# The opening of a two-layer diffusion trunk on one core: the first pair of projection tiles moved ahead of the second block's modulation sums, the third tile computed beside them

## The chip, the core and the metric

The kernel runs on one core of one Trainium2 chip. The metric is device time in microseconds (us) for one execution of the whole program; the time before is the median of three runs. Five engines each work through an instruction queue of their own and wait for one another by semaphores: TensorE (PE, matmuls; PEld is its weight load), VectorE (DVE), ScalarE (ACT), GpSimd (POOL) and SyncE (SP, which issues most of the DMAs).

## What is computed

One inference step of a trunk of two layers (`DEPTH` 2) over 128 context tokens and 512 latent tokens, with 1024 features, in float32. The part that matters here is the start of the first layer:

```python
def trunk_layer(x, cond, ctx_k, ctx_v, p):
    sh1, sc1, gt1, sh2, sc2, gt2 = modulation(cond, p['w_mod'], p['b_mod'])
    h = rms_norm(x, p['norm1_g']) * (1.0 + sc1) + sh1
    q, k, v, u = mixer_projections(h, p['w_in'], p['q_norm_g'], p['k_norm_g'])
...
def modulation(cond, w_mod, b_mod):
    m = jax.nn.silu(cond) @ w_mod + b_mod
    return jnp.split(m[:, None, :], N_MOD, axis=-1)
...
def mixer_projections(h, w_in, q_norm_g, k_norm_g):
    proj = h @ w_in
...
```

After it come attention, a pooling mixer, an output projection and a gated MLP; then the second layer, and a final norm.

## The kernel before

Features lie on the partitions: `x` is 8 blocks k of 128 features by 640 tokens. A projection is made in tiles of 128 output features. The input projection of a layer has 10 tiles: four of u (tiles 0 to 3), then k, v and four of q. Each float32 operand is split into a high and a low part, and a product is made of three: high by high, low weights by high input, high weights by low input. For one block k and one tile each of them is two matmuls, of 384 and 256 tokens ("a product" below is such a pair of matmuls).

ACT makes the high part of the weights (`w_hi`, by `hi`, L658) and DVE the low part (`w_lo`, by `lo`, L1027), from the raw weights (`w_raw`, two slots, filled by SP). `w_hi` and `w_lo` have two slots as well: the parts of tile n+2 replace those of tile n, so `hi` of tile n+2 waits until tile n is finished. Tile 2 has a place of its own in memory that the attention uses later (`k_hi`, `k_lo`).

The opening of layer 0 works like this.

- PE transposes the tokens of `x` (L1742) into two PSUM places, DVE and ACT copy the results out. ACT sums squares, and PE spreads the reciprocal root mean square of each token over the partitions (L1629). DVE multiplies `x` by it, block by block (`scaled_x`, L1200).
- The shift and the scale of the norm come from 8 MB of weights, in 4 blocks f of 256 features of each. For a block PE makes the sums in two halves (`first_sums(f, h)`, L1703, a block's half needs 1 MB of weights, `w_first`, loaded in two DMAs), ACT copies the row (L784), PE turns it into columns (`first_columns(f)`, L1714), and DVE adds these up to the shift and gain of features 2f and 2f+1 (`first_mod(f)`, L1206 to L1212). Only then can ACT make the normed input of these two blocks k (L797, "sq", then its high part `in_hi`, L801) and DVE the low part (`in_lo`, L1232).
- PE then makes tiles 0 and 1 together (`linear_pair`): for each k the high products, then the low ones, with the sums of later blocks in between and `first_columns(k//2+1)` in the middle of k = 0, 2 and 4. Tile 2 follows alone (`linear_third`), then the first of eight small steps for other modulations (`mod_second(0)`, L1720), then tile 3 (`linear`, L1468) and on.

SP issues the loads in the order of the program: tokens, block 0 of `w_first`, tiles 0 and 1, blocks 1 to 3, tiles 2 and 3, constants.

Of the kernel before, what the change touches and what calls it, by code (L numbers as in the profile page):

```python
# [21 lines left out]
P = 128  # L22
# [39 lines left out]
def build(nc, x_prompt, x_sample, cache_k, cache_v, c, c_ctx, w_mod, b_mod, norm1_g, w_in,  # L62
# [72 lines left out]
    with ExitStack() as ctx:  # L135
# [15 lines left out]
        cst = sb("cst", [P, n_const])  # L151
        ident, head_ones, ones = (cst[:, i * P:(i + 1) * P] for i in range(3))
        cos, sin = (cst[:, 3 * P + i * TS:3 * P + (i + 1) * TS] for i in range(2))
        fold = cst[:, n_const - P:n_const]
        edge = cst[:, 3 * P + 2 * TS:n_const - P].rearrange("p (g s e c) -> p g s e c", g=NPOOL, s=2, e=2)
# [4 lines left out]
        eps = sb("eps", [P, 2])  # L160
        wp = sb("wp", [P, NPOOL, P])
# [25 lines left out]
        XE_SCALAR, XE_VECTOR = [4, 6], [0, 1, 2, 3, 5, 7]  # L187
# [77 lines left out]
        s_xhat = sem("x_scaled")  # L265
# [104 lines left out]
        def own_place(n):  # L370

            t = n % PER_LAYER
            if t == 2:
                return w_third_in
            return w_own_up[2 * (t - N_IN - N_OUT):2 * (t - N_IN - N_OUT) + 2]

# [14 lines left out]
        def _(sp):  # L391
# [25 lines left out]
            def load_second(k):  # L417
                if k == 0:
                    sp.wait_ge(s_xsq, NT)
                elif k == 1:  # L420
                    sp.wait_ge(s_fcol, NK // 2)
                else:
                    sp.wait_ge(s_second, k - 1)
# [22 lines left out]
            sp.dma_start(cst[:, P:n_const - P], consts[:, P:n_const - P]).then_inc(s_const, 16)  # L446
            load_second(0)
            load_second(1)
            for L in range(DEPTH):
# [79 lines left out]
        def _(pool):  # L529
# [32 lines left out]
            pool.memset(cond_cols, 0.0).then_inc(s_c32z, 1)  # L562
            for L in range(DEPTH):
# [14 lines left out]
                if L == 0:  # L578
                    pool.wait_ge(s_const, 16)
# [22 lines left out]
                for e in range(NE):  # L602
                    E = L * NE + e
                    tgt = keys[:, TP + PAST:TP + PAST + TS] if e == 0 else qk[:, e % 3, TP:T]
                    if E > 0:
                        pool.wait_ge(s_qk, E)
                    pool.wait_ge(s_shuf, E + 1)
# [44 lines left out]
        def _(act_e):  # L652
# [7 lines left out]
            def slot_loads(n, s):  # L660
                return n // 2 + 1 if isinstance(n, int) else (n - s) // 2 + 1

            def hi_own(n):

                s = n % 2
                act_e.wait_ge(s_raw[s], 16 * slot_loads(n, s))
                act_e.activation(own_place(n)[0], w_raw[:, s, 0:NK, :], ACT.Copy).then_inc(s_whi, 1)

            def hi_at(base, i, s, nk):

                act_e.wait_ge(s_raw[s], 16 * (i + (base // 2 + 1)))
# [99 lines left out]
            act_e.activation(rtok[:, :], rtok[:, :], ACT.Sqrt, bias=eps[:, 0:1], scale=1.0 / D).then_inc(s_sd, 1)  # L771
            for k in XE_SCALAR:
                act_e.wait_ge(s_xt, k + 1)
                act_e.activation(x[:, k, :], pair[k % 2][:, 0:T], ACT.Copy).then_inc(s_xe, 1)
            hi(0, 0, NK)


            for k in range(NK):
                if k == 0 or k % 2 == 1 and k + 1 < NK:
                    f = (k + 1) // 2  # L780
                    act_e.wait_ge(s_mfirst, f + 1)
                    if f >= 2:
                        act_e.wait_ge(s_fcol, f - 1)
                    act_e.activation(first_rows[:, f % 2, :], pair[2][:, f % 2 * 512:(f % 2 + 1) * 512], ACT.Copy).then_inc(s_frow, 1)  # L784
                if k == 0:
                    for L in range(DEPTH):
                        act_e.wait_ge(s_vec_t, L + 2)
                        for t in range(3):
                            ins = act_e.activation(vec[:, L, t, 0:N_ROWS[t]], pair[L][:, t * P:t * P + N_ROWS[t]], ACT.Copy)
                        ins.then_inc(s_vec, 1)  # L790
                    hi(1, 1, NK)
# [1245 lines left out]
```

## Time and profile before

| | us |
|---|---|
| median of 3 runs | 1442.25 (1441.65 to 1442.99) |
| span of the profiled execution, first to last instruction | 1439.4 |
| start of the first product of the projection | 29.87 |
| start of tile 3 | 59.86 |

The profile shows one execution. Its own time is known as the span; the 2.85 us by which the median exceeds it lie around the first and last instruction. Times in the trace count from the first instruction. A busy PE there is not PE at its peak, since matmuls overlap.

### The profile page before, as it was taken

The numbers are of one execution on the slowest core, as the hardware profiler recorded it, in microseconds if no ns is written. First come the engines' busy times: TensorE is split into PE (matmuls) and PEld (weight loads), VectorE is DVE, ScalarE is ACT, GpSimd is POOL, SyncE is SP. The second block draws the span as 40 slices with busy tenths as digits, with TensorE's granted clock in tenths as the row PEclk, the third lists the DMA queues.
The fourth block names the chain that finished last, engine by engine and source line by source line (L and its number), as shares of the span: only waits on it lengthen the run. The fifth ranks groups of instructions, "written<-read, shape, count | busy, mean of one in ns | idle before, by whom it ended". The sixth has DMA issues, their size and how long they took to land.

```text
span 1439.4 us, 25053 instructions
## 1 busy us (share of the span) xinstructions
PE 1407.3 (98%) x9905; PEld 1353.2 (94%) x9905; DVE 903.1 (63%) x1429; ACT 534.1 (37%) x798; POOL 400.5 (28%) x273
## 2 busy tenths in 40 slices
PE   6999999999999999999999999999999999999997
PEld 4888889999999999999999977999999999999997
DVE  4448869897966478785775787369744323444333
ACT  5436862533231123232242587344233112232322
POOL 0264002153440033433205800214433101323321
PEclk9999999999999999999999999999999999999999
DMA  9752005253535334335423200224323312222321
GB/s 315 248 178 80 1 2 161 81 166 106 164 121 162 94 117 145 120 120 153 120 58 86 63 1 2 59 89 132 104 79 90 87 57 67 73 73 73 101 61 74
DMA packets 198158, 147.05 MB, mean 102 GB/s; under 512 B 4400, under 2 KB 187448, under 8 KB 197048
## 3 DMA queue, kind: packets, MB, share of 16 engines
q1 hardware_dynamic: 196592, 144.27, 32.8%
q10 hardware_dynamic: 1480, 1.57, 0.3%
q8 instruction: 61, 1.00, 0.3%
q14 instruction: 25, 0.20, 0.0%
HBM read 142.94 MB, written 2.88 MB: 101 GB/s over the span
## 4 chain that ended last, share of the span: by engine, by line
PE 87%; DVE 7%; ACT 2%; issue 2%; SPq 1%; DMA 1%; DVEq 0%; ACTq 0%
PE pair L1468 68%; PE pair L1484 7%; PE pair L1865 3%; PE pair L1910 3%; PE pair L1879 2%; DVE mod_acc L1050 1%; DVE in_lo L1116 1%; DVE norm_t L1106 1%; SPq L414 1%; DVE conv L1390 1%; DMA w_first<-in_w_mod_dram 1%; DVE w_lo L1027 1%; DVE small L1328 1%; PE pair L1768 1%; PE pair L1720 1%
## 5 line engine op out<-in xcount | busy, mean ns | idle before, releaser
L1468 PE MATMUL pair<-in_hi,w_hi 128*128 128x384 f32 x1728 | 396.1, 310 | 0.2
L1468 PE MATMUL pair<-in_lo,w_hi 128*128 128x384 f32 x1728 | 394.7, 309 | 0.0
L1468 PE MATMUL pair<-in_hi,w_lo 128*128 128x384 f32 x1728 | 392.7, 308 | 0.0
L1390 DVE SCALAR_TENSOR_TENSOR conv<-pair,vec,conv 128x127 f32<-128x127 f32 x352 | 168.7, 541 | 193.4 <-ACT conv L935 192.9
L1468 PEld LDWEIGHTS pair<-in_hi,w_hi 128*128 128x128 f32 x1728 | 265.4, 189 | 5.6 <-issue 2.2
L1468 PEld LDWEIGHTS pair<-in_lo,w_hi 128*128 128x128 f32 x1728 | 265.6, 189 | 0.0
L1468 PEld LDWEIGHTS pair<-in_hi,w_lo 128*128 128x128 f32 x1728 | 263.6, 188 | 0.0
L636 POOL TENSOR_TENSOR silu_a<-silu_a,conv 128x640 f32<-128x640 f32 x44 | 113.0, 2567 | 534.2 <-DVE conv L1390 534.2
L935 ACT ACTIVATE conv<-pair,vec 128x640 f32<-128x640 f32 x88 | 77.8, 886 | 407.5 <-PE pair L1468 405.3
L1027 DVE TENSOR_TENSOR w_lo<-w_raw,w_hi 128x1024 fp32r<-128x1024 f32 (+1 forms) x148 | 195.7, 1322 | 38.4 <-ACT w_hi L658 37.9
L658 ACT ACTIVATE w_hi<-w_raw 128x1024 fp32r<-128x1024 f32 (+1 forms) x82 | 96.9, 1182 | 287.1 <-PE pair L1468 270.5
L1050 DVE SCALAR_TENSOR_TENSOR mod_acc<-mod_raw,cond,mod_acc 128x1024 f32<-128x1024 f32 x112 | 181.5, 1666 | 0.0
L1183 DVE SCALAR_TENSOR_TENSOR x<-pair,mod,x 128x128 f32<-128x128 f32 x80 | 40.3, 545 | 165.4 <-PE pair L1468 165.4
L1468 PE MATMUL pair<-act_lo,w_hi 128*128 128x384 f32 x616 | 140.7, 309 | 0.0
L1468 PE MATMUL pair<-act_hi,w_hi 128*128 128x384 f32 x616 | 140.3, 309 | 0.0
L1468 PE MATMUL pair<-act_hi,w_lo 128*128 128x384 f32 x616 | 140.1, 308 | 0.0
L547 POOL TENSOR_TENSOR ssum<-ssum,sq 128x640 f32<-128x640 f32 x24 | 48.6, 2025 | 300.7 <-ACT sq L682 300.7
L1468 PEld LDWEIGHTS pair<-act_lo,w_hi 128*128 128x128 f32 x616 | 94.8, 189 | 0.0
L1468 PEld LDWEIGHTS pair<-act_hi,w_hi 128*128 128x128 f32 x616 | 94.5, 188 | 0.0
L1468 PEld LDWEIGHTS pair<-act_hi,w_lo 128*128 128x128 f32 x616 | 94.1, 188 | 0.0
L640 POOL TENSOR_TENSOR act_lo<-silu_a,act_hi 128x640 f32 x44 | 84.4, 1918 | 7.5 <-POOL act_hi L638 7.5
L673 ACT ACTIVATE w_hi<-w_raw 128x1024 fp32r<-128x1024 f32 x64 | 67.2, 1050 | 0.0
(205 smaller groups left out, 1775.5 us busy)
## 6 DMA issues: line engine op xcount, KB each, us to landing
w_raw<-in_w_up_dram SPq DMA_DIRECT2D x88, 512.0 KB, 3.8
mod_raw<-in_w_mod_dram SPq DMA_DIRECT2D x64, 512.0 KB, 4.4
w_raw<-in_w_down_dram SPq DMA_DIRECT2D x32, 704.0 KB, 4.6
w_raw<-in_w_in_dram SPq DMA_DIRECT2D x20, 512.0 KB, 4.2
w_first<-in_w_mod_dram SPq DMA_DIRECT2D x16, 512.0 KB, 8.8
w_raw<-in_w_out_dram SPq DMA_DIRECT2D x16, 512.0 KB, 4.1
mod_raw<-in_w_mod_dram SPq DMA_DIRECT2D x4, 1024.0 KB, 5.1
mod_acc<-in_w_mod_dram SPq DMA_DIRECT2D x4, 1024.0 KB, 5.0
```

Source lines behind the costliest of these rows:

```text
L547: pool.tensor_tensor(ssum[:, :], ssum[:, :], sq_slot(m), ALU.add).then_inc(s_ss, 1)
L636: pool.tensor_tensor(silu_a[:, :], silu_a[:, :], conv[:, 1, :], ALU.mult).then_inc(s_act, 1)
L640: pool.tensor_tensor(act_lo[:, j, :], silu_a[:, :], act_hi[:, j, :].bitcast(F32), ALU.subtract).then_inc(s_alo, 1)
L658: act_e.activation(w_hi[:, s, 0:nk, :], w_raw[:, s, 0:nk, :], ACT.Copy).then_inc(s_whi, 1)
L673: act_e.activation(w_hi[:, s, 0:nk, :], w_raw[:, s, 0:nk, :], ACT.Copy).then_inc(s_whi, 1)
L935: act_e.activation(conv[:, s, :], up_result(g, j, s), ACT.Identity, bias=v(L, V_CONVB, s * NF + g * FG + j), scale=v(L, V_TAP[1], s * NF + ...
L1027: dve.tensor_tensor(w_lo[:, s, 0:nk, :], w_raw[:, s, 0:nk, :], w_hi[:, s, 0:nk, :].bitcast(F32), ALU.subtract).then_inc(s_wlo, 1)
L1050: dve.scalar_tensor_tensor(out=mod_acc[:, ci, :], in0=mod_raw[:, s, :], scalar=cond[:, ci, ds(k, 1)], in1=mod_acc[:, ci, :], op0=ALU.mult, ...
L1390: ins = dve.scalar_tensor_tensor(out=conv[:, s, d0:d1], in0=up_result(g, j, s)[:, d0 + sh:d1 + sh], scalar=v(L, V_TAP[t], s * NF + g * FG ...
L1468: ins = pe.matmul(dst[:, a:e], w[:, s, k, :], rhs[:, kk, a:e], start=first and r == 0, stop=last and r == 2)
L1484: ins = pe.matmul(dst[:, a:e], w, rhs[:, a:e], start=start, stop=stop)
L1865: ins = pe.matmul(lin[i % 2][:, oc:oc + n], q_st[:, h, b * P:(b + 1) * P], kk[:, h // GRP, kc:kc + n], start=r == 0, stop=r == 1)
```

## The change

The work of the first 60 us is put in another order, and some of it into other places. No arithmetic is removed but for the filler matmuls, which become 12 instead of 6.

- **Loads.** Tile 2's raw weights go to a place of their own (half of `mod_raw`) and are issued behind block 1 of `w_first`, ahead of blocks 2 and 3. Its two parts (`third_hi`, `third_lo`) lie where the rotation tables (`turn`) and the past keys and pool weights lie later, so these loads wait for the end of tile 2.
- **Transposes.** Three PSUM places instead of two; the sums of block 0 and the first half of the vectors stand between and behind the last transposes, ahead of the spreading of the norm. ACT copies the spread norm to `spread_x`, and `scaled_x` reads it there.
- **Weights.** GpSimd makes the high part of tile 1. On DVE the low part of tile 0 comes behind `first_mod(0)`, that of tile 1 behind the first `in_lo`, that of tile 2 behind `first_mod(1)`.
- **PE.** k = 0 of tiles 0 and 1 comes ahead of both halves of block 1's sums; then k = 1 with `first_columns(1)` in its middle; then k = 0 and 1 of tile 2; from k = 2 on the three tiles go together, with `first_columns(2)` and `first_columns(3)` in the middle of k = 3 and k = 5. Behind k = 7 come at once `mod_second(0)` and tile 3.
- **PSUM.** Sums of blocks 1 to 3 lie in `pair[3]` instead of `pair[2]`, which tile 2 now needs.

```diff
@@ SP
-            for f in range(1, NK // 2):
+            sp.wait_ge(s_xsq, 4)
+            load_first(1)
+            sp.dma_start(third_raw, w_in_v[0][:, :, IN_COLUMN[2]:IN_COLUMN[2] + P]).then_inc(s_third, 16)
+            for f in range(2, NK // 2):
                 load_first(f)
-            for n in range(2, 4):
-                load_in(0, n)
...
+            load_in(0, 3)
...
+            sp.wait_ge(s_lin, 3)
+            sp.dma_start(turn[:, :], consts[:, 3 * P:3 * P + 2 * TS]).then_inc(s_turn, 16)
@@ GpSimd
+            pool.wait_ge(s_raw[1], 16)
+            pool.wait_ge(s_whi, 1)
+            pool.tensor_copy(w_hi[:, 1, 0:NK, :], w_raw[:, 1, 0:NK, :]).then_inc(s_whi, 1)
@@ ScalarE
+            first_copied(0)
+            act_e.wait_ge(s_bc, 1)
+            act_e.activation(spread_x, lin[3], ACT.Copy).then_inc(s_spread, 1)
             hi(0, 0, NK)
+            vec_copied(1)
...
+                if k % 2 == 1 and k + 1 < NK:
+                    first_copied((k + 1) // 2)
+                if k == 1:
+                    hi_own(2)
@@ VectorE
-            dve.wait_ge(s_bc, 1)
-            for k in range(2):
-                scaled_x(k)
-            lo(0, 0, NK)
+            dve.wait_ge(s_spread, 1)
+            scaled_x(0)
...
             first_mod(0)
-            lo(1, 1, NK)
+            lo(0, 0, NK)
+            scaled_x(1)
             for k in range(NK):
+                dve.wait_ge(s_hhi, 2 * (k + 1))
+                dve.tensor_tensor(in_lo[:, k, :], sq[:, k % 2, :], in_hi[:, k, :].bitcast(F32), ALU.subtract).then_inc(s_h, 2)
+                if k == 0:
+                    lo(1, 1, NK)
                 if k + 2 < NK:
                     scaled_x(k + 2)
                 if k % 2 == 1 and k + 1 < NK:
                     first_mod((k + 1) // 2)
...
+                if k == 1:
+                    lo(2, 0, NK)
...
-                    if L == 0 or n > 0:
+                    if n > 0:
                         lo(N + 2, n % 2, NK)
@@ TensorE
+            first_sums(0, 1)
             pe.wait_ge(s_rstd, 1)
+            x_emptied(5)
             spread_tiles(range(NT)).then_inc(s_bc, 1)
...
             first_columns(0)
+            vec_turned(1)
...
+            keep_busy(12, pair[0][:, 0:P])
...
-                    linear_pair(tile_in(L), NK, in_hi, in_lo, *h_wait(2 * L), first_ahead, first_between)
-                    linear_third(tile_in(L) + 2, NK, in_hi, in_lo, lin[2])
+                    opened_hi(0, (0, 1))
+                    opened_lo(0, (0, 1))
+                    first_sums(1, 0)
+                    first_sums(1, 1)
+                    opened_hi(1, (0, 1))
+                    first_columns(1)
+                    opened_lo(1, (0, 1))
...
+                    for k in range(2):
+                        opened_hi(k, (2,))
+                        opened_lo(k, (2,))
+                    first_sums(2, 0)
+                    opened_hi(2, (0, 1, 2))
+                    opened_lo(2, (0, 1, 2))
+                    first_sums(2, 1)
+                    opened_hi(3, (0, 1, 2))
+                    first_columns(2)
+                    opened_lo(3, (0, 1, 2))
+                    first_sums(3, 0)
+                    opened_hi(4, (0, 1, 2))
+                    opened_lo(4, (0, 1, 2))
+                    first_sums(3, 1)
+                    opened_hi(5, (0, 1, 2))
+                    first_columns(3)
+                    opened_lo(5, (0, 1, 2))
+                    for k in range(6, NK):
+                        opened_hi(k, (0, 1, 2))
+                        opened_lo(k, (0, 1, 2))
+                    pe.wait_ge(s_fsum, NK // 2)
                     mod_second(0)
```

`opened_hi(k, tiles)` makes the two products with the high input of each tile, and waits at k = 0 for the low part of that tile's weights; `opened_lo` makes the one with the low input, and at k = 7 tells that the tile is finished.

**Where the order moves.** First, PE's queue at the last columns (block 3; the names are PSUM place, then input and weights, then the shape; in brackets the semaphores waited for). Before, in the middle of k = 4:

```order
L1714 MATMUL pair2<-cst,mod_acc 128x128 [waits first_rows_copied]
L1714 MATMUL pair2<-cst,mod_acc 128x128 x3
L1484 MATMUL pair0<-in_lo,w_hi 128x384 [waits h_ready]
L1484 MATMUL pair0<-in_lo,w_hi 128x256
L1484 MATMUL pair1<-in_lo,w_hi 128x384
L1484 MATMUL pair1<-in_lo,w_hi 128x256
L1484 MATMUL pair0<-in_hi,w_hi 128x384 [waits h_hi_ready]
```

Now, in the middle of k = 5:

```order
L1741 MATMUL pair3<-cst,mod_acc 128x128 [waits first_rows_copied]
L1741 MATMUL pair3<-cst,mod_acc 128x128 x3
L1541 MATMUL pair0<-in_lo,w_hi 128x384 [waits h_ready]
L1541 MATMUL pair0<-in_lo,w_hi 128x256
L1541 MATMUL pair1<-in_lo,w_hi 128x384
L1541 MATMUL pair1<-in_lo,w_hi 128x256
L1541 MATMUL pair2<-in_lo,third_hi 128x384
L1541 MATMUL pair2<-in_lo,third_hi 128x256
L1541 MATMUL pair0<-in_hi,w_hi 128x384 [waits h_hi_ready]
```

The last row of the first piece is k = 5, whose features come from block 2; that of the second is k = 6, whose features come from these very columns.

Second, DVE's queue from the spreading of the norm to the low part of tile 1 (`xin` is the scaled `x`; L1200 is now L1254, L1027 is L1081, L1232 is L1281). Before:

```order
L1200 TENSOR_TENSOR xin<-x,pair3 128x640 [waits x_evacuated_by_vector,rstd_spread]
L1200 TENSOR_TENSOR xin<-x,pair3 128x640 [waits x_evacuated_by_vector]
L1027 TENSOR_TENSOR w_lo<-w_raw,w_hi 128x1024 [waits w_hi_ready]
L1221 SCALAR_TENSOR_TENSOR first_gain<-vec 128x8 [waits vec_ready]
L1206 TENSOR_REDUCE first_sum<-pair2 128x8 [waits first_columns_done,first_gain_ready]
```

Now:

```order
L1254 TENSOR_TENSOR xin<-x,v_feat 128x640 [waits x_evacuated_by_vector,rstd_copied]
L1273 SCALAR_TENSOR_TENSOR first_gain<-vec 128x8 [waits vec_ready]
L1260 TENSOR_REDUCE first_sum<-pair2 128x8 [waits first_columns_done,first_gain_ready]
...
L1081 TENSOR_TENSOR w_lo<-w_raw,w_hi 128x1024 [waits w_hi_ready]
L1254 TENSOR_TENSOR xin<-x,v_feat 128x640 [waits x_evacuated_by_vector]
L1281 TENSOR_TENSOR in_lo<-sq,in_hi 128x640 [waits h_hi_ready]
L1081 TENSOR_TENSOR w_lo<-w_raw,w_hi 128x1024 [waits w_hi_ready]
```

The second row of L1081 is the low part of tile 1; it now has one scaling, `first_mod(0)`, the low part of tile 0, a second scaling and the first low input ahead of it.

Third, DVE's queue behind the last low input, where the tiles of u are copied out of PSUM (L1294 and L1295, now L1351 and L1352) and the low part of tile 3 is made. Before:

```order
L1294 COPY u<-pair0 128x128 [waits pads_cleared,lin_done]
L1295 COPY u<-pair0 128x512
L1025 TENSOR_TENSOR k_lo<-w_raw,k_hi 128x1024 [waits w_hi_ready]
L1294 COPY u<-pair1 128x128 [waits lin_done]
L1295 COPY u<-pair1 128x512
L1027 TENSOR_TENSOR w_lo<-w_raw,w_hi 128x1024 [waits w_hi_ready]
```

Now:

```order
L1351 COPY u<-pair0 128x128 [waits pads_cleared,lin_done]
L1352 COPY u<-pair0 128x512
L1351 COPY u<-pair1 128x128 [waits lin_done]
L1352 COPY u<-pair1 128x512
L1081 TENSOR_TENSOR w_lo<-w_raw,w_hi 128x1024 [waits w_hi_ready]
```

L1025, tile 2's low part, has left this place; the last row, tile 3's low part, still follows the copies of tiles 0 and 1. Before, PE had all of tile 2 to do after those two tiles were finished; now the three are finished together.

## Rows read from the trace of the kernel before

**Rows 1.** The page: the chain that ended last, its shares by engine.

```profile
PE 87%; DVE 7%; ACT 2%; issue 2%; SPq 1%; DMA 1%; DVEq 0%; ACTq 0%
```

**Rows 2.** Chain in order of time, opening: start us, us, what.

```profile
22.87 10.00 DMA w_first<-in_w_mod_dram
...
43.89 1.20 ACT sq L797 x2
...
45.17 0.75 ACT in_hi L801
...
45.96 12.98 PE pair L1484 x84
```

**Rows 3.** Timeline, PE: start us, us, operation; in brackets idle before, releaser.

```profile
24.18 1.60 PE L1654 MATMUL pair<-cst 128*128 128x128 f32 x12
...
28.87 1.06 PE L1703 MATMUL pair<-w_first,ssum 128*32 128x512 f32 x8 [1.94 <-DMA w_first<-in_w_mod_dram]
29.87 0.56 PE L1484 MATMUL pair<-in_hi,w_hi 128*128 128x384 f32 x2
...
32.91 1.07 PE L1703 MATMUL pair<-w_first,ssum 128*32 128x512 f32 x8 [0.55 <-DMA w_first<-in_w_mod_dram]
...
39.30 1.06 PE L1703 MATMUL pair<-w_first,ssum 128*32 128x512 f32 x8
...
42.26 1.07 PE L1703 MATMUL pair<-w_first,ssum 128*32 128x512 f32 x8
...
44.54 0.60 PE L1714 MATMUL pair<-cst,mod_acc 128*128 128x128 f32 x4
...
45.96 0.56 PE L1484 MATMUL pair<-in_hi,w_hi 128*128 128x384 f32 x2 [0.23 <-ACT in_hi L801]
...
51.73 0.46 PE L1484 MATMUL pair<-in_hi,k_hi 128*128 128x384 f32 x2
...
58.87 1.06 PE L1720 MATMUL pair<-mod_raw,ssum 128*32 128x512 f32 x8
59.86 0.56 PE L1468 MATMUL pair<-in_hi,w_hi 128*128 128x384 f32 x2
```

**Rows 4.** Timeline, DVE, columns as in rows 3.

```profile
20.73 1.55 DVE L1200 TENSOR_TENSOR xin<-x,pair 128x640 f32<-128x640 f32 x2 [0.29 <-PE pair L1629]
...
24.28 0.19 DVE L1206 TENSOR_REDUCE first_sum<-pair 128x8 f32<-128x32 f32 x1 [0.47 <-PE pair L1714]
...
25.15 1.22 DVE L1027 TENSOR_TENSOR w_lo<-w_raw,w_hi 128x1024 fp32r<-128x1024 f32 x1
...
45.17 0.19 DVE L1206 TENSOR_REDUCE first_sum<-pair 128x8 f32<-128x32 f32 x1 [1.97 <-PE pair L1714]
...
45.54 0.28 DVE L1212 TENSOR_SCALAR gain<-first_sum,vec,first_gain 128x2 f32<-128x2 f32 x1
...
51.63 0.29 DVE L1294 COPY u<-pair 128x128 f32<-128x128 f32 x1 [0.90 <-PE pair L1484]
...
52.44 1.22 DVE L1025 TENSOR_TENSOR k_lo<-w_raw,k_hi 128x1024 fp32r<-128x1024 f32 x1
...
54.37 1.52 DVE L1027 TENSOR_TENSOR w_lo<-w_raw,w_hi 128x1024 fp32r<-128x1024 f32 x1
```

**Rows 5.** Timeline, ACT: a copy of 640 tokens from PSUM.

```profile
18.59 0.70 ACT L774 ACTIVATE x<-pair 128x640 f32<-128x640 f32 x1 [0.85 <-PE pair L1742]
```

**Rows 6.** Groups by form, POOL: the nearest copies; xcount | busy us, mean ns | idle before.

```profile
L638 POOL CAST act_hi<-silu_a 128x640 f32 x44 | 45.6, 1036 | 7.3 <-POOL silu_a L636 7.3
```

**Rows 7.** Timeline, POOL: the first window sum.

```profile
52.70 2.11 POOL L591 TENSOR_TENSOR tree<-u 128x663 f32<-128x663 f32 x1 [9.04 <-DVE u L1295]
```

**Rows 8.** Stretch 25 to 30 us: PE, PEld, DVE, ACT, POOL busy, clock, DMA share, GB/s.

```profile
25.00:30.00 5.00, 2.98 (x25) 1.04 (x24) 3.65 (x6) 1.90 (x4) 0.00 (x0) 1.00 1.09 348
```

**Rows 9.** The page: DMA issues, KB each, us to landing.

```profile
w_raw<-in_w_in_dram SPq DMA_DIRECT2D x20, 512.0 KB, 4.2
```

More of the change, by code:

```diff
@@ L160, in build @@
         eps = sb("eps", [P, 2])
+        with ExitStack() as own:
+            third_lo = sb("third_lo", [P, NK, P], F32R, at=own)
         wp = sb("wp", [P, NPOOL, P])
@@ L606, in _ @@
                         pool.wait_ge(s_qk, E)
+                    else:
+                        pool.wait_ge(s_turn, 16)
                     pool.wait_ge(s_shuf, E + 1)
@@ L1734, in x_emptied, with vec_turned @@
                     pe.wait_ge(s_xe_dve, XE_VECTOR.index(k) + 1)
+            def vec_turned(L):
+                if L > 0:
+                    pe.wait_ge(s_vec, L)
+                for t in range(3):
+                    ins = pe.transpose(vec_place(t), rows[0:N_ROWS[t], L, t, :], ident[0:N_ROWS[t], 0:N_ROWS[t]])
+                ins.then_inc(s_vec_t, 1)
+            N_ROW_DMAS = 5 + 4 + 3 + DEPTH
             for k in range(NK):
-                if k >= 2:
-                    x_emptied(k - 2)
+                if k >= 3:
+                    x_emptied(k - 3)
                 for b in range(NT):
@@ L1790, in _, with opened_hi @@
-                    linear_pair(tile_in(L), NK, in_hi, in_lo, *h_wait(2 * L), first_ahead, first_between)
-                    linear_third(tile_in(L) + 2, NK, in_hi, in_lo, lin[2])
+                    opening = [(lin[s], w_hi[:, s, :, :], w_lo[:, s, :, :]) for s in range(2)] + [(lin[2], third_hi, third_lo)]
+                    def opened_hi(k, tiles):
+                        pe.wait_ge(s_hhi, 2 * (k + 1))
+                        for t in tiles:
+                            if k == 0:
+                                pe.wait_ge(s_wlo, t + 1)
+                            dst, w, l = opening[t]
+                            product(dst, w[:, k, :], in_hi[:, k, :], k == 0, False)
+                            product(dst, l[:, k, :], in_hi[:, k, :], False, False)
@@ new lines, in opened_lo @@
+                    def opened_lo(k, tiles):
+                        pe.wait_ge(s_h, 2 * (k + 1))
+                        for t in tiles:
+                            dst, w, _ = opening[t]
+                            ins = product(dst, w[:, k, :], in_lo[:, k, :], False, k == NK - 1)
+                            if k == NK - 1:
+                                ins.then_inc(s_lin, 1)
+                    opened_hi(0, (0, 1))
+                    opened_lo(0, (0, 1))
+                    first_sums(1, 0)
```

149 lines of the change are left out of this document (65 added, 84 removed).

## The prediction

> **What bounds the kernel now.** I read the page's chain first: 87% of it is PE [rows 1], so what counts is when PE gets through its queue, and a delay in the opening goes to the end unless something later takes it up. The chain in order of time then shows the first 60 us: up to 32.9 us the loads of the modulation weights end last, at 43.89 and 45.17 ACT's making of a feature block, and from 45.96 PE alone without a break [rows 2]. PE's timeline gives the sizes. Its first product of the projection is at 29.87, because the second half of block 1's sums waited 1.94 us for its weights; there are 0.55 and 0.23 us more of waiting behind it; tile 3 starts at 59.86 [rows 3]. So about 2.7 us of visible waiting can be won there, besides the filler in front of it (1.60 us [rows 3]), and the question is what the new order waits for instead.
>
> **What is only moved.** All products, sums and columns remain, so PE has the same work from the first product to tile 3, plus the two halves of block 1's sums, which now stand behind the first product. Twelve fillers instead of six (3.2 us instead of 1.60 [rows 3]) stand where PE waits for ACT anyway and end before 26.2 (below); without that cover they would delay the first product. I set tile 3's start against 59.86. Behind it the queues are as before. Unit prices: tile 2 alone took from 51.73 to 58.87 for 24 products, 0.2975 each. One half of sums with a pair's k (6 products) took 39.30 to 42.26, so 1.175 for the sums [rows 3].
>
> **The start.** Before, DVE could scale from 20.73 [rows 4]. Now the spread stands behind both halves of block 0's sums, which were behind it: 2.35 later if nothing else changes, and none later if the third PSUM place removes as much waiting from the transposes. Neither is in the trace; I take the middle, 21.9 (20.7 to 23.1). ACT's copy adds 0.70 [rows 5] and a step of 0.05: 22.65. Then DVE works in a row: scaling 0.78 (half of 1.55), `first_mod(0)` 0.87 (24.28 to 25.15), low part of tile 0 1.22, scaling 0.78, the first low input, taken as 0.78 too, low part of tile 1 1.22 [rows 4]. That ends at 28.30. Meanwhile the first feature is ready 0.65 into `first_mod` (45.17 to 45.54 and 0.28 [rows 4]), at 24.1, and ACT needs 2.07 from there to PE's product (43.89 to 45.96 [rows 2]). **The first product comes at 26.2 instead of 29.87**, but after tile 0's two (0.6) PE must wait until 28.35 for tile 1: **wait of 1.55**. GpSimd's high part of tile 1, which no row shows, is an estimate of 1.66 from 1.036 for 640 columns [rows 6]; it starts behind ACT's high part of tile 0 at some 23.7 and is wanted at 27.1, so it could take twice as long and cost nothing.
>
> **k = 0 and 1.** From 28.35 come 4 products (to 29.54), two halves of sums (31.89), 4 products (33.08), the columns of block 1. Behind columns DVE starts 0.63 after PE's start (44.54 to 45.17 [rows 3, 4]), takes 0.87, and only then makes the low part of tile 2, 1.22: 35.85. PE has 0.6 of columns and 0.6 of products to do, until 34.3: **wait of 1.55**. The raw weights of tile 2 are no part of it: block 1 is there at 28.87 [rows 3], 0.5 MB at 348 GB/s [rows 8] is 1.5 more, and ACT asks for them after 32.
>
> **k = 2 to 7.** Tile 2's k = 0 and 1 (37.63), sums (38.81), k = 2 of three tiles, 9 products, 2.68 (41.49), sums (42.66), 6 products (44.45), columns of block 2. Now the price of having columns directly ahead of the k that needs them: 0.63 to DVE, 0.65 to the first gain, 0.04, and 2.07 over ACT: **3.39 us** from the start of the columns to the next high product. Before, a whole k and a half of sums lay between. At k = 4 PE has columns, 3 low products and sums to do, 2.67: **wait of 0.7**, until 47.84. k = 4 (50.52), sums (51.69), 6 products (53.48), columns of block 3. Here only columns and 3 low products cover, 1.5: **wait of 1.9**, until 56.87. k = 6 and 7, 5.36: the three tiles end at 62.22. Blocks 2 and 3 of the weights come 1.5 us later than before, behind tile 2's; PE asks for block 2 at 37.6 where it was there at 32.9, and for the last half at 50.5 where it did not wait at 42.26 [rows 3]. That part works: no DMA is waited for any more.
>
> **The end of the opening.** The slot of tile 3 is free only when tile 1 ends, 0.3 before the end. DVE has the copies of tiles 0 and 1 ahead of tile 3's low part, 0.81 each (51.63 to 52.44 [rows 4]), from 0.55 before the end to 1.07 after it, then the low part. It took 1.52 there and 1.22 elsewhere [rows 4]; I take 1.52, since GpSimd's window sum starts there too. ACT's high part lies beside the copies. PE has only `mod_second(0)` in the meantime, 0.99 (58.87 to 59.86 [rows 3]), where before it had tile 2, 7.1: **wait of 1.65**. Tile 3 starts at 62.22 + 2.64 = 64.86.
>
> **Sum.** 64.86 against 59.86: 5.0 us later. Five new waits of 7.4 together stand against the 3.7 by which the first product comes earlier, of which the moved sums take back 2.35. Of the remaining first 100 us the one risk is tile 4's weights: their load now stands behind tables, past keys and pool weights (0.9 MB) that wait for the end of tile 2. At 348 GB/s [rows 8] that is 2.6, and 4.2 for the load itself [rows 9], so some 7 after the end, 9.3 with both parts; PE asks at 10.8. It is hidden, with 1.5 to spare. Span 1439.4 + 5.0 = 1444.4; with the 2.85 that lie around it, **1447.2 us**. The bounds: the start moves everything by 1.2 either way, tile 3's low part at 1.22 takes 0.3 off, and sums at 1.0 each (28.87 to 29.87 [rows 3]) instead of 1.175 another 0.9 over the five that are on the path.
>
> **A rule weighed.** The low part of tile 3 began at 54.37, while GpSimd's sum ran from 52.70 to 54.81, and took 1.52 instead of 1.22 [rows 4, 7]: 0.3 more, which the sum has. The Trainium skill (SBUF — State Buffer, section "Who interferes with whom") says that a VectorE instruction with two SBUF inputs and a GpSimd instruction that reads SBUF exclude each other, the later one being blocked entirely. By that, the trace agrees in kind but not in size: blocked until 54.81, it would have ended 0.44 + 1.22 after its start, 1.66.
>
> **Rivals.** *GpSimd blocks DVE.* Tile 0's low part would start when GpSimd's copy ends (25.3 instead of 24.3), and tile 3's when a window sum of 2.11 [rows 7], started 0.3 after the end, is over: 1.0 more at each, +7.0, 1449.2. The one case in the trace shows a third of that. *About no change.* The start at its early bound, with 1.2, 0.3 and 0.9 less: +2.6, 1444.9. For it: the transposes do have waits that a third place removes. Against it: the longest waits hang on chains that do not depend on the start. *Faster.* The one thing that would turn the sign is the chain behind columns: if a feature block followed its columns within the 1.5 us that PE has to do in every case, and the low parts were as quick, there would be no new waits, and 3.7 - 2.35 + 0.78 is 2.1 gained, 1440.1; with the early start 3.3, 1439.0. Against it stand 3.39 measured link by link, all of them instructions that no part of the change shortens.
>
> **How the numbers follow.** Differences of less than 0.2% (2.9 us) can't be told from none. The forecast, 1445.2 to 1448.8: 0.62. Blocking, up to some 1449.5: 0.13. About no change, 1439.4 to 1445.1: 0.19. Faster than that: 0.06. Slower thus has 0.75. The range for 8 in 10, 1444.2 to 1449.3, takes in the early start and most of the blocking.
>
> **What the changed profile would show.** First product near 26.2 and no DMA named as a releaser of L1730. PE idle before tile 1's first product (about 1.5, released by DVE's low part), before tile 2's first (1.5, the same), before k = 4 (0.7) and k = 6 (1.9, released by ACT's `in_hi`), and before tile 3 (1.6, DVE's low part). Tile 3 starting near 64.9. I am wrong if the spread is ready well before 21 us, if `in_hi` of k = 6 comes within 2.5 us of the columns, or if what follows tile 3 gives time back.

## The result and the profile after

The changed kernel is slower: median 1453.62 us of five runs (1452.5 to 1454.28) against 1441.65 for the kernel before on the same chip (1439.98 to 1442.99); ratio 1.0084, 95% interval 1.0072 to 1.0096. That is 12 us. The profiled execution took 1453.45, its span 1451.4 us against 1439.4. The direction was forecast; 5.0 us were forecast, and 12 lie outside the range.

PE's timeline of the changed kernel, from the same places as [rows 3] (start, busy time, line, operation, operands, count; in brackets the idle time in front and what ended it):

```profile
12.79 5.78 PE L1777 MATMUL pair<-cst,xin 128*128 128x128 f32 x26 [1.24 <-DMA xin<-in_x_sample_dram]
28.68 0.56 PE L1541 MATMUL pair<-in_hi,w_hi 128*128 128x384 f32 x2 [1.51 <-ACT in_hi L853]
30.75 0.56 PE L1541 MATMUL pair<-in_hi,w_hi 128*128 128x384 f32 x2 [1.21 <-DVE w_lo L1081]
38.16 0.54 PE L1541 MATMUL pair<-in_hi,third_hi 128*128 128x384 f32 x2 [1.69 <-DVE third_lo L1079]
50.20 0.56 PE L1541 MATMUL pair<-in_hi,w_hi 128*128 128x384 f32 x2 [0.92 <-ACT in_hi L853]
59.31 0.87 PE L1541 MATMUL pair<-in_hi,w_hi 128*128 128x384 f32 x2 [1.92 <-ACT in_hi L853]
59.98 0.73 PE L1541 MATMUL pair<-in_hi,w_lo 128*128 128x384 f32 x2
66.33 1.07 PE L1747 MATMUL pair<-mod_raw,ssum 128*32 128x512 f32 x8
69.42 0.70 PE L1525 MATMUL pair<-in_hi,w_hi 128*128 128x384 f32 x2 [2.03 <-DVE w_lo L1081]
79.17 0.56 PE L1525 MATMUL pair<-in_hi,w_hi 128*128 128x384 f32 x2
```

Read the brackets first. The DMA waits of [rows 3] are gone, and the five forecast waits are all there, with the forecast releasers: 1.21, 1.69, 0.92, 1.92, 2.03, together 7.8 (forecast 7.35). The 1.51 at 28.68 is the making of the first feature, which the forecast had in the time of the first product. So the list of waits is right, and yet the first product comes at 28.68, not 26.2, and tile 3 starts at 69.42, not 64.86. Now read the durations: the same two-instruction row takes 0.46 us at most places, and 0.70 to 0.87 behind the waits at 59.31 and 69.42. The table by stretches says why; the column that matters is PEclk, the granted clock of TensorE as a share of full speed:

```profile
core 0: us, PE busy (x) PEld busy (x) DVE busy (x) ACT busy (x) POOL busy (x), PEclk, DMA share, GB/s
55.00:59.30 4.30, 2.40 (x18) 2.13 (x16) 0.93 (x5) 1.98 (x4) 0.00 (x0) 1.00 0.43 118
59.30:62.70 3.40, 3.39 (x13) 3.39 (x14) 1.65 (x2) 1.79 (x3) 0.00 (x0) 0.51 0.38 161
62.80:66.30 3.50, 3.50 (x25) 3.33 (x23) 0.45 (x2) 0.08 (x1) 0.00 (x0) 1.00 0.00 0
69.70:73.00 3.30, 3.30 (x14) 3.30 (x14) 0.38 (x1) 0.00 (x0) 0.12 (x1) 0.50 0.99 287
```

Half speed is the lower of TensorE's two clocks, 1.2 instead of 2.4 GHz. PE issued 13 and 14 matmuls in stretches in which it issues about 25 at full speed. Each of them begins right behind a wait of PE (1.92 and 2.03 us). The kernel before shows 1.00 from 16 to 80 us. The price of the two can be read from the starts: k = 6 and 7 take 7.02 us (59.31 to 66.33) instead of the forecast's 5.36, and tile 3 with its `mod_second` 9.75 (69.42 to 79.17) instead of the 8.25 that they take in the kernel before (59.86 to 68.11): 1.7 and 1.5 more. A third such stretch lies in the second layer's attention (0.53 at 837.4 to 840.8) and costs nothing that lasts: PE is 12.05 late in front of it and 12.0 at the end.

A second thing is the start itself. PE's timeline from the last tile of `x` to the spreading of the norm (L1629, now L1656), first of the kernel before, then of the changed one with VectorE's first scaling:

```profile
12.58 5.97 PE L1742 MATMUL pair<-cst,xin 128*128 128x128 f32 x31 [1.12 <-DMA xin<-in_x_sample_dram]
18.81 0.77 PE L1742 MATMUL pair<-cst,xin 128*128 128x128 f32 x5 [0.26 <-DVE x L1190]
19.41 1.28 PE L1629 MATMUL pair<-cst,rtok 128*128 128x128 f32 x10
```

```profile
18.39 0.55 PE L1767 MATMUL pair<-cst,rows 114*128 114x114 f32 x3
18.87 1.06 PE L1730 MATMUL pair<-w_first,ssum 128*32 128x512 f32 x8
19.87 1.31 PE L1777 MATMUL pair<-cst,xin 128*128 128x128 f32 x10
21.11 1.07 PE L1730 MATMUL pair<-w_first,ssum 128*32 128x512 f32 x8
22.11 1.38 PE L1656 MATMUL pair<-cst,rtok 128*128 128x128 f32 x10
24.26 0.82 DVE L1254 TENSOR_TENSOR xin<-x,v_feat 128x640 f32<-128x640 f32 x1 [2.76 <-ACT v_feat L838]
```

The 36 transposes behind the landing of the last tile take 6.8 us in both kernels, waits included. So the third PSUM place gave nothing back; the waiting that the trace of the kernel before shows there is 0.26. The two halves of sums and the first vectors, 2.5 us that now stand ahead of the spread, delay it by their full length.

A third thing stands on VectorE and GpSimd (timeline of the changed kernel):

```profile
25.32 1.04 POOL L602 CAST w_hi<-w_raw 128x1024 fp32r<-128x1024 f32 x1 [24.20 <-ACT w_hi L700]
25.42 0.95 DVE L1263 TENSOR_SCALAR mod<-first_sum,vec 128x2 f32<-128x2 f32 x1
26.48 0.22 DVE L1263 TENSOR_SCALAR mod<-first_sum,vec 128x2 f32<-128x2 f32 x1
66.91 1.29 POOL L631 TENSOR_TENSOR tree<-u 128x663 f32<-128x663 f32 x1 [12.46 <-DVE u L1352]
67.45 1.83 DVE L1081 TENSOR_TENSOR w_lo<-w_raw,w_hi 128x1024 fp32r<-128x1024 f32 x1
```

The same instruction on 2 elements takes 0.95 us while GpSimd's copy runs, ending with it (26.36), and 0.22 after it. Tile 3's low part, begun while GpSimd's window sum runs, takes 1.83. And far behind the opening, in the second layer, a fourth: two rows of VectorE and one of PE, first of the kernel before, then of the changed one.

```profile
783.40 1.23 DVE L1027 TENSOR_TENSOR w_lo<-w_raw,w_hi 128x1024 fp32r<-128x1024 f32 x1 [4.05 <-ACT w_hi L658]
823.39 0.18 DVE L1334 TENSOR_TENSOR small<-small,rq 128x1 f32<-128x1 f32 x1
824.20 0.44 PE L1865 MATMUL pair<-k_hi,q_st 128*128 128x384 f32 x1 [0.69 <-ACT sq L896]
```

```profile
792.90 2.94 POOL L631 TENSOR_TENSOR tree<-tree 128x657 f32<-128x657 f32 x2
794.44 2.49 DVE L1081 TENSOR_TENSOR w_lo<-w_raw,w_hi 128x1024 fp32r<-128x1024 f32 x1 [4.42 <-ACT w_hi L700]
834.33 1.28 POOL L650 TENSOR_TENSOR rope<-rope,turn 128x512 f32<-128x512 f32 x1
834.43 1.19 DVE L1391 TENSOR_TENSOR small<-small,rq 128x1 f32<-128x1 f32 x1
836.25 0.44 PE L1932 MATMUL pair<-k_hi,q_st 128*128 128x384 f32 x1 [1.24 <-ACT sq L950]
```

Up to there the changed kernel is 11.04 late (833.31 against 822.27 for VectorE's instruction ahead of it); behind the attention's first product it is 12.05 late (836.25 against 824.20), and so it stays to the end. The `w_lo` row that takes 2.49 instead of 1.23 thus costs nothing at its own place; the 1.0 us is the row on one element at 834.43, which begins just after GpSimd and ends with it.

### The profile page after: what moved, and what is told of

Same layout as the page of the kernel before. It is cut to its first block, busy times and chain, and to the rows that moved or that the text cites. A ratio compares the mean times of both kernels' runs of the same rounds, so it can differ in the third digit from the quotient of the medians.

```text
span 1451.4 us, 25120 instructions
## 1 busy us (share of the span) xinstructions
PE 1413.3 (97%) x9917; PEld 1360.4 (94%) x9917; DVE 907.8 (63%) x1428; ACT 534.7 (37%) x799; POOL 401.8 (28%) x274
## 4 chain that ended last, share of the span: by engine, by line
PE 87%; DVE 8%; ACT 2%; issue 2%; DMA 1%; SPq 0%; DVEq 0%; ACTq 0%
PE pair L1525 68%; PE pair L1541 7%; PE pair L1932 3%; PE pair L1977 3%; PE pair L1946 2%; DVE mod_acc L1104 1%; DVE in_lo L1170 1%; DVE norm_t L1160 1%; DVE w_lo L1081 1%; DVE conv L1447 1%; DVE small L1385 1%; DMA xin<-in_x_sample_dram 1%; PE pair L1803 1%; PE pair L1777 0%; PE pair L1730 0%
## 5 line engine op out<-in xcount | busy, mean ns | idle before, releaser
L1081 DVE TENSOR_TENSOR w_lo<-w_raw,w_hi 128x1024 fp32r<-128x1024 f32 (+1 forms) x148 | 198.8, 1343 | 41.3 <-ACT w_hi L700 41.0
```

Source lines behind the costliest of these rows:

```text
L1081: dve.tensor_tensor(w_lo[:, s, 0:nk, :], w_raw[:, s, 0:nk, :], w_hi[:, s, 0:nk, :].bitcast(F32), ALU.subtract).then_inc(s_wlo, 1)
```

## The experiments

Theory T1: the forecast waits cost what was forecast, and what is missing is TensorE's clock, which falls where PE stands still. Rival T2: only the waits cost, and what is missing lies in them or elsewhere. The kernels of e1 to e4 shared one chip, as did e5 to e8 and e9 to e11; each ratio is against the kernel before, run beside them. Differences below are differences of ratios times 1441 us; all of them are under 1%, so the intervals decide which can be told apart. Places in the trace are of one execution, in which the last tile of `x` was there at some time between 11.58 and 12.79 us.

| kernel | median us | ratio, 95% interval |
|---|---|---|
| the change | 1453.62 | 1.0084 (1.0072 to 1.0096) |
| e1 waits filled | 1450.40 | 1.0061 (1.0047 to 1.0075) |
| e2 early spare matmuls | 1452.94 | 1.0080 (1.0066 to 1.0094) |
| e3 early columns | 1446.93 | 1.0038 (1.0024 to 1.0051) |
| e4 tile 2 last | 1451.36 | 1.0069 (1.0055 to 1.0083) |
| e5 kernel before, early spare matmuls | 1443.11 | 1.0009 (1.0001 to 1.0018) |
| e6 = e3 + e2 | 1445.85 | 1.0034 (1.0021 to 1.0047) |
| e7 = e3 + early copy | 1446.38 | 1.0036 (1.0023 to 1.0049) |
| e8 all repairs | 1443.17 | 1.0013 (1.0004 to 1.0022) |
| e9 = e1 + e2, orders unchanged | 1448.92 | 1.0059 (1.0045 to 1.0072) |
| e10 = e8 + tile 4's weights first | 1440.61 | 0.9998 (0.9989 to 1.0007) |
| e11 = e10 + GpSimd behind VectorE | 1439.25 | 0.9988 (0.9979 to 0.9997) |
| e12 = e11 without early spare matmuls | 1440.01 | 0.9989 (0.9980 to 0.9998) |

**e1, waits filled with spare matmuls.** The results of these matmuls are used by nobody.

```diff
+                        if k == 6:
+                            keep_busy(7, pair[3][:, 0:P])
...
+                    FILL = {1: 4, 2: 6}
...
+                            if k == 0 and t > 0:
+                                keep_busy(FILL[t], pair[3][:, 0:P])
...
                     mod_second(0)
+                    keep_busy(8, pair[3][:, 0:P])
```

> The changed kernel with spare matmuls (each 128 columns, into a free part of the fourth pair of banks) put into four of the waits that it showed: 4 before tile 1's first product, 6 before tile 2's first product, 7 before k = 6, 8 before tile 3. They take less time than the waits, so nothing else moves. T1 (the clock falls because TensorE stands still): no half-clock stretch at 59 and at 70 us, the matmuls there take 0.46 instead of 0.73 us, tile 4 starts 3.2 us earlier (75.9 instead of 79.2), and the time is 1449 to 1450.5. T2 (only the waits cost): the waits stand as fillers, time 1453.6, as the change.

3.3 us faster than the change. PE's timeline of e1, and its granted clock where the change fell to half:

```profile
56.60 1.72 PE L1681 MATMUL pair<-cst 128*128 128x128 f32 x14
58.67 0.56 PE L1541 MATMUL pair<-in_hi,w_hi 128*128 128x384 f32 x2 [0.35 <-ACT in_hi L853]
59.07 0.46 PE L1541 MATMUL pair<-in_hi,w_lo 128*128 128x384 f32 x2
```

```profile
58.60:62.00 3.40, 3.33 (x22) 3.33 (x23) 1.65 (x2) 1.85 (x4) 0.00 (x0) 1.00 0.40 169
67.20:70.60 3.40, 3.35 (x24) 3.37 (x24) 0.72 (x2) 0.00 (x0) 0.46 (x3) 1.00 0.93 268
```

PE gets its `in_hi` no earlier than before (1.72 of fillers and 0.35 of waiting instead of 1.92), but what follows runs at full clock. From the first product to tile 4 it takes 47.33 us (28.14 to 75.47) against 50.49 in the change: 3.2 less, the price of the two stretches. Work that does nothing made the kernel faster: that is T1, and T2 falls for these 3 us.

**e2, early spare matmuls.** The aim was the slow transposes at 12.79 (in the kernel before 31 of them take 5.97).

```diff
                     if k == 0:
+                        keep_busy((6, 1, 1, 1, 2)[b], pair[2][:, 2 * P:3 * P])
                         pe.wait_ge(s_x[b], 16)
```

> The changed kernel with 11 spare matmuls while TensorE waits for the five tiles of x (4 to 12.8 us). T1: the full clock is there when the last tile of x lands, the transposes take about 0.11 us each instead of 0.213 from the start, the rstd copy on ScalarE comes at 21.5 to 22 instead of 23.5, the first product at about 26.7 instead of 28.7: time 1451.6, with the half-clock stretches at 59 and 70 us still there. Rival: the start is set by the copies and the DMA, the first product stays within 0.5 us: 1453.2 to 1453.6.

A miss in time. In the profile the 26 transposes take 3.47 us instead of 5.78, the first product comes at 26.33, and 2.35 reach the end of that execution, which was the fastest of five; but 0.97 of it is that `x` landed earlier (11.82 against 12.79). The median gained 0.6, within the interval. Nor do the spare matmuls always quicken the transposes: in e6, e9 and e11, which have them too, the 26 take 4.25 to 4.51, with a granted clock of 0.50 between 12.5 and 14.2. That the clock makes them slow in the change is not shown: the granted clock in its profile is 1.00 there. Both half-clock stretches were still there, as expected.

**e3, early columns**: the two halves of a block's sums together ahead of k = 2 and k = 4, its columns one k earlier; the diff shows block 2, block 3 is moved alike.

```diff
                     first_sums(2, 0)
+                    first_sums(2, 1)
                     opened_hi(2, (0, 1, 2))
+                    first_columns(2)
                     opened_lo(2, (0, 1, 2))
-                    first_sums(2, 1)
                     opened_hi(3, (0, 1, 2))
-                    first_columns(2)
                     opened_lo(3, (0, 1, 2))
```

> The changed kernel with both halves of block 2's sums before k = 2 and its columns behind k = 2's high products, block 3's one k earlier in the same way (sums before k = 4, columns in k = 4): the chain columns, copy, sums, gain, sq, in_hi then lies beside 3.5 us of products. T1: the waits of 0.92 at k = 4 and 1.92 at k = 6 shrink under 0.3 each, and without the second there is no half-clock stretch at 59 us (1.6 more): 4.0 to 4.4 us less, 1449.4. T2: 2.5 us less, 1451.1. If the blocks' DMA is late (37.2 and 43.2 us landed), the gain is under 1.5.

6.6 us faster than the change, more than either theory gave. PE's timeline:

```profile
48.60 0.57 PE L1541 MATMUL pair<-in_hi,w_hi 128*128 128x384 f32 x2
54.46 0.46 PE L1541 MATMUL pair<-in_hi,w_hi 128*128 128x384 f32 x2
62.93 0.53 PE L1525 MATMUL pair<-in_hi,w_hi 128*128 128x384 f32 x2 [2.03 <-DVE w_lo L1081]
63.30 0.46 PE L1525 MATMUL pair<-in_lo,w_hi 128*128 128x384 f32 x2
```

k = 4 and k = 6 have no wait left. The wait before tile 3 is as long as it was, 2.03, but behind it the rows stay at 0.46: the same single wait, and no fall of the clock. So the length of one wait doesn't decide. From the first product to tile 4 it takes 43.57 us (27.56 to 71.13) against 50.49, 6.9 less: 2.84 of waits, 3.2 of the two half-clock stretches, and 0.9 that was not traced. Later in this execution 1.4 are lost again (see Open).

**e4, tile 2 last**: at k = 6 and 7 tiles 0 and 1 first.

```diff
-                    for k in range(6, NK):
-                        opened_hi(k, (0, 1, 2))
-                        opened_lo(k, (0, 1, 2))
+                    for tiles in ((0, 1), (2,)):
+                        for k in range(6, NK):
+                            opened_hi(k, tiles)
+                            opened_lo(k, tiles)
```

> The changed kernel with k = 6 and 7 of tiles 0 and 1 first and of tile 2 last, so that 1.8 us of products lie between tile 1's end and tile 3, in which tile 3's weights are split. The wait of 2.03 before tile 3 shrinks to 0.2 to 0.6. T1: the half-clock stretch at 70 us goes with it (1.6 more), 3 to 3.4 us less, 1450.4. T2: 1.4 to 1.8 less, 1452.0.

2.2 us faster than the change, between the two, so the time can't decide. The wait is 0.56 and the stretch behind it runs at full clock, as T1 says, but this execution had a half-clock stretch where the change had none, behind the second of two early waits:

```profile
28.69 0.90 PE L1541 MATMUL pair<-in_hi,w_hi 128*128 128x384 f32 x2 [1.21 <-DVE w_lo L1081]
29.39 0.73 PE L1541 MATMUL pair<-in_hi,w_lo 128*128 128x384 f32 x2
67.36 0.53 PE L1525 MATMUL pair<-in_hi,w_hi 128*128 128x384 f32 x2 [0.56 <-DVE w_lo L1081]
```

The wait of 1.21 is the same in both, one time followed by 0.46, the other by 0.73. Which wait is followed by a fall differs from execution to execution.

**e5, the kernel before with the early spare matmuls of e2.**

> The kernel before with the same 11 spare matmuls while TensorE waits for the tiles of x. T1: the clock rises early here too, and the transposes take about 0.11 us each from the start, but the first product waits for block 1's DMA (landed 28.83 in the trace of before) whatever the clock was, so the wait before it grows from 1.94 by what the start saves: time 1441.4 to 1441.8, no gain. Rival (an early clock is worth the same in both kernels): 2 us less, 1439.7.

Neither: it became slower, by 1.3 us. PE's timeline and granted clock:

```profile
29.21 1.94 PE L1703 MATMUL pair<-w_first,ssum 128*32 128x512 f32 x8 [2.81 <-DMA w_first<-in_w_mod_dram]
31.78 0.74 PE L1484 MATMUL pair<-in_hi,w_lo 128*128 128x384 f32 x2
```

```profile
15.60:29.00 13.40, 10.12 (x77) 6.36 (x76) 9.76 (x17) 7.24 (x16) 0.00 (x0) 1.00 1.12 332
29.20:32.50 3.30, 3.29 (x13) 1.63 (x14) 0.00 (x0) 1.29 (x3) 0.00 (x0) 0.50 1.09 348
```

As expected the earlier start only lengthens the DMA wait, 2.81 instead of the 1.94 of [rows 3]; not expected was that the clock then falls behind it. Behind the opening PE is 1.2 us late in this execution; 1.4 more are lost near 990 us (see Open), so how the 1.3 of the median divides is not shown. The fall of the clock, though, belongs to no new layout or order: the kernel before has it too once it waits longer.

**e6, e3 and e2 together.**

> The kernel of the early columns and the early spare matmuls together. T1: no half-clock stretch is left to move about, the first product comes 2 us earlier than with the early columns alone, and the end too: 1444.9 (1444.5 to 1445.5). Rival: the start doesn't carry to the end, as it did not in the median of the early spare matmuls alone (0.7 of 2.4): 1446.3.

Inconclusive: the median of 1445.85 lies between the two, and the interval takes in both. A half-clock stretch was there after all, at 28.2 to 31.5 (granted clock 0.50), at the waits of 1.51 and 1.21.

**e7, e3 with GpSimd's copy started when the tile has landed.**

```diff
             pool.wait_ge(s_raw[1], 16)
-            pool.wait_ge(s_whi, 1)
             pool.tensor_copy(w_hi[:, 1, 0:NK, :], w_raw[:, 1, 0:NK, :]).then_inc(s_whi, 1)
```

> The kernel of the early columns, and GpSimd's copy of tile 1's high part starts when the tile has landed (about 22 to 23 us) instead of behind ScalarE's copy of tile 0, so that it no longer runs while VectorE makes the first modulation. If the two engines shut each other out there, that modulation takes 0.23 instead of 0.95 us, the first in_hi and the first product come 0.7 us earlier: 1446.2. If the 0.95 has another cause, nothing moves: 1446.9.

The low part of tile 0 on VectorE then waits for both high parts. VectorE's timeline shows the cause:

```profile
25.16 0.23 DVE L1262 TENSOR_SCALAR mod<-first_sum,vec 128x2 f32<-128x2 f32 x1
```

With the copy at 22.58, the row is 0.23, and ACT's wait behind it 0.31 instead of 1.03; from the landing of x to the first product it is 15.3 us instead of 16.0 in e3. The end time can't tell (1.0036 against 1.0038, within the intervals).

**e8, all repairs at once**: e3, e4, the early copy, the early spare matmuls, the low part of tile 1 ahead of the second scaling, those of tile 2 ahead of block 1's row copy and modulation, `mod_second(1)` ahead of tile 3.

> Early columns, early spare matmuls and early copy as before; tile 1's low part made ahead of the second scaling on VectorE; third tile's high part ahead of block 1's row copy on ScalarE and its low part ahead of block 1's modulation on VectorE; k = 6 and 7 of tile 2 last; the second mod_second ahead of tile 3. T1: every one of the five waits is under 0.4, no half-clock stretch before 800 us, tile 4 at 64 to 65 instead of 79.2 us (68.1 before): 1438 to 1440, faster than the kernel before by 2 to 3. If the waits were only moved or the DMA of block 2 binds, 1442 to 1444.

A miss, 1.9 slower than the kernel before. After the first product PE has one wait over 0.6 left in the opening, and it is one that the prediction had called hidden:

```profile
68.41 0.53 PE L1523 MATMUL pair<-in_hi,w_hi 128*128 128x384 f32 x2 [1.63 <-DVE w_lo L1080]
```

Tile 4's weights wait in SP's queue behind `turn`, which waits for three finished tiles; in the change PE was so late that this cost nothing. There is also a half-clock stretch at 28.1 to 31.4 (0.50); the waits ahead of it are 1.62 and, with four rows at full speed between, 0.56. With this and the wait at tile 4 the opening gains nothing; what makes this execution slower than the kernel before lies outside it: PE is 0.2 us late at 144 us, 1.6 late behind 299 (see Open) and 2.6 late behind the second layer's attention.

**e9, the orders of the change, with spare matmuls only** (those of e1 and e2, and 17 instead of 12 ahead of the first product).

> The changed kernel with every order as it was and spare matmuls alone: 11 while the tiles of x land, 17 instead of 12 ahead of the first product, and the 25 in the four waits. The five waits stay in place, filled. T1 (the prediction had the waits right and left the clock out): the full clock from about 8 us to the attention of the second layer, the first product at 26.3, tile 4 at 73.2 to 73.6, and the time 1447.5 to 1448.5, next to the 1447.2 that was predicted. Rival (the missing 6 us are something else): above 1449.5.

0.4 above T1's bounds and 0.6 under the rival's; the first product came at 27.08, not 26.3. PE's timeline and clock:

```profile
74.47 0.56 PE L1525 MATMUL pair<-in_hi,w_hi 128*128 128x384 f32 x2
```

```profile
15.60:80.00 64.40, 62.12 (x448) 51.10 (x447) 31.83 (x59) 26.60 (x45) 9.27 (x16) 1.00 0.81 251
```

At full clock the same five waits bring tile 4 at 74.47. The prediction's tile 4 is 73.1 (64.86 and the 8.25 that tile 3 and its `mod_second` take at full clock); the change's is 79.17. This execution and that of the change differ by 4.70, of which 1.60 are there at the first product (27.08 against 28.68; 0.33 of it is when `x` landed) and 3.1 are the two stretches.

**e10 and e11.** e10 is e8 with `load_in(0, 4)` ahead of the wait for three tiles in SP's queue, and 18 fillers ahead of the first product. e11 adds one wait to it:

```diff
+                        if L == 1 and g == 3 and r == 3:
+                            pool.wait_ge(s_wlo, tile_in(L) + IN_K + 4)
```

> All repairs, and tile 4's weights ahead of the table turn, past and wp in SyncE's queue (there they came behind the wait for three finished tiles and landed at 65.9 us, 1.6 us too late), and 18 spare matmuls ahead of the first product instead of 12. T1: no wait over 0.6 after the first product and no half-clock stretch before 800 us; tile 4 at 66.2 instead of 68.4 us, 1440 to 1441 (the collisions of VectorE and GpSimd at 294 and 784 us, 1.3 and 1.0, are in it): the same as the kernel before. Rival (DMA binds the opening): tile 4 still waits for its weights, 1442.5 to 1443.2.

> The kernel of e10_repairs_turn, and in the second layer the last step of GpSimd's fourth window sum waits until VectorE has made tile 7's low part, which is the order that the kernel before shows (VectorE at 783.40, GpSimd at 783.59). If the 1.0 us at the start of the second layer's attention comes from who takes the shared port first, w_lo takes 1.23 instead of 2.49 there, the wait at the first attention is 0.7 instead of 1.24, and the time is 1.0 less than that kernel: 1439 to 1440. If not, no difference.

Both as expected. e10 takes the same time as the kernel before, with no wait left at tile 4. e11 is 1.4 us faster than e10 (the intervals overlap, so the rows below carry the reading) and 1.7 faster than the kernel before, the only kernel here, with e12, whose interval lies under 1. In the profiled executions PE is 1.6 (e10) and 1.9 us (e11) ahead of the kernel before behind the opening; at the end e10 is 0.7 late, e11 still 1.9 ahead. Its timeline, at the places of the second layer shown above:

```profile
781.52 1.23 DVE L1084 TENSOR_TENSOR w_lo<-w_raw,w_hi 128x1024 fp32r<-128x1024 f32 x1 [4.42 <-ACT w_hi L703]
821.51 0.18 DVE L1393 TENSOR_TENSOR small<-small,rq 128x1 f32<-128x1 f32 x1
822.33 0.44 PE L1938 MATMUL pair<-k_hi,q_st 128*128 128x384 f32 x1 [0.69 <-ACT sq L953]
```

In e10 the three are 2.49, 1.15 and 1.24, as in the change: a wait on GpSimd's queue gives all of them back.

**e12, e11 without the early spare matmuls.**

> The kernel of e11_pool_order without the 11 spare matmuls while the tiles of x land. T1: the clock rises later, x's transposes take about 0.2 us each, the first product comes 1.5 to 2.3 us later in relation to the last tile of x; block 2's DMA, for which that kernel still waits 0.3, takes some of it back: 1 to 2 us more, 1440.3 to 1441.3, 0.2 to 0.8 under the kernel before. Rival (an early clock only brings the first fall forward, as the kernel before with the early spare matmuls suggests, which became 2 us slower): no difference, 1.8 under the kernel before.

The rival holds: 1.0 (0.9989 against 0.9988) is not lost. In this execution the transposes took 4.70 instead of 5.78 without any help. The early spare matmuls are worth nothing in this kernel.

## Why the prediction was wrong in size

Right were, step by step: no DMA is waited for any more; the five waits, each at its place, with its releaser and within 0.4 us; the 3.39 from a block's columns to the next high product (3.40 and 3.39 in the changed kernel); tile 4's weights hidden in the changed kernel (e8 shows how narrowly); the sign. Where the rest came in:

| us | forecast | measured | later than forecast |
|---|---|---|---|
| first product | 26.2 | 28.68 | 2.5 |
| k = 6 | 56.87 | 59.31 | 2.4 |
| end of the three tiles | 62.22 | 66.33 | 4.1 |
| tile 3 | 64.86 | 69.42 | 4.6 |
| tile 4 (64.86 and 8.25) | 73.11 | 79.17 | 6.1 |
| behind the second layer's attention | | | 7.1 |

Two steps failed by much, and neither explains the miss alone: without the first the change would be 8.8 slower, without the second 9.6, and the range ended at 7.1.

The first, 3.2 us, is the unit price. "All products, sums and columns remain, so PE has the same work" holds for instructions, and the prices (0.2975 a product, 1.175 a half of sums) came from a stretch of the kernel before in which the clock was full throughout. The five waits were entered as 7.4 us of standing still and nothing else. At two of them the work behind the wait then ran at half the clock, 1.7 and 1.5 more. e1 shows it by filling the waits, e3 by taking two of them away; in e9, with the waits in place and the clock kept up, the kernel is 3.6 us faster than the change (ratios 1.0059 and 1.0084), its earlier first product included.

The Trainium skill (TensorE: Matmul & The Clock Gate, section "A second HAM failure mode: psum-queue depth-cycling") describes a kernel in which TensorE idles briefly between groups of matmuls often enough for its clock to go to and fro. That kernel is another one, which goes round its PSUM banks in each iteration; what this trace shares with it is the outcome: 0.51 at 59.3 and 0.50 at 69.7 us, behind waits of 1.92 and 2.03. No run here shows that the cause is the same.

The second, 2.5 us at the first product and 2.4 behind it, is the start: 26.2 forecast, 28.68 measured. "Neither is in the trace; I take the middle" put half of the 2.35 down as won back by the third PSUM place. Nothing was won back, and the first vectors, which now stand ahead of the spread too, were left out: VectorE scales from 24.26 instead of 22.65, 1.6 later. Another 0.7 is the modulation that took 0.95 beside GpSimd's copy (e7), and 0.2 `first_gain`, which now stands in front of it. The copy took 1.04 where the estimate was 1.66, so its price was no danger, but where it ran was; the rival "GpSimd blocks DVE" was right in kind and looked at the low parts only. That the spread is late for these reasons is read from the rows; no run moved the sums back.

Tile 3 adds 0.4: its wait is 2.03 instead of 1.65, since its low part took 1.83 beside GpSimd's window sum where 1.52 was entered.

Outside the opening 1.0 came at the second layer's attention, which the prediction had ruled out with "Behind it the queues are as before". They are; but VectorE and GpSimd met in another order. The Trainium skill (SBUF — State Buffer, section "Who interferes with whom") says that it is the order of issue that decides which of the two is blocked; e11 agrees: VectorE first, 1.23; GpSimd first (in e10 and the change), 2.49. The later order follows from this one: with it put right, the row on one element takes 0.18 again.

The account of the profiled execution: 5.0 as predicted, 2.4 of the start, 3.2 of the two stretches, 0.4 at tile 3 and 1.0 in the second layer are 12.0, and the spans differ by 12.0.

**Open.** Which of several equal waits is followed by a fall of the clock (not the one at 30.75 in the change, but the one at 28.69 in e4) is not explained by any row. Nor is why the order in the second layer turned: in the kernel before, VectorE begins tile 6's low part at 777.32, 0.47 after ACT's high part has ended, in the changed one 0.1 after it; that lets GpSimd's sums start earlier. e3, e4, e8 and e10 show another such meeting near 294 us, and e1 and e5 one near 990, where VectorE's `mod_acc` takes 2.6 instead of 1.3 and PE then waits 1.4; it was not taken apart, and the medians of these kernels hold an unknown share of it.

## What to carry to other kernels

A wait can cost more than its length when the engine that waits is TensorE: sum the waits of an opening, then ask at what clock the work behind them will run, and give a price at the lower clock as the other bound (here 1.5 and 1.7 us for the two falls). Where a wait in the middle of the work can't be removed, fill it with matmuls that nobody needs (e1: 3.3 us; spare matmuls at the very start were worth nothing in e12); where it can, put the products of one k between a chain's start and its end (e3: 6.6 us from four moved lines). Before a delay is put down as half won back, look for the waiting that could be won: here the trace of the kernel before had 0.26 of it. When a change shifts one of VectorE and GpSimd against the other, look through the whole program for the places where they start within a few tenths of a microsecond of each other: an order that happened to be good can be fixed by one wait.

## What the runs showed of the hardware that was not expected

- A VectorE instruction on 2 elements took 0.95 us instead of 0.23 while GpSimd copied 128x1024 float32 (e7 took the overlap away). One on a single element took 1.19 instead of 0.18 beside GpSimd's rotation (e11).
- TensorE's granted clock fell to half at waits of 0.56 (e8), 1.21 (e4), 1.92 and 2.03 (the change) and 2.81 us (e5), not always at the same one: 1.21 in the change, 1.94 in the kernel before and 2.03 in e3 were not followed by a fall.
- GpSimd's copy of 128x1024 float32 with rounding took 1.04 us, as long as ACT's (1.05).
